# One-core hybrid decoder step: TensorE's implied waits dropped or moved, and ScalarE's bias writes moved ahead of the casts

## The chip, the cores and the metric

The kernel runs on one core of one Trainium2 chip. The metric is the device time of one execution in microseconds (us). Before the change, three runs gave a median of 1390.84 us, from 1389.94 to 1391.01.

## What is computed

One layer of a decoder for 512 prompt tokens and 8 x 4 sample tokens (544 rows of 1024 columns): windowed attention, a short convolution and memory cross-attention, an output projection, and then a mixture of 32 experts of which each token takes 4. All data is float32. The change lies in the experts alone. For the tokens of one expert the reference does this:

```
h = xb @ w_gate_up[e] + b_gate_up[e]          # 1024 -> 2048, gate and up interleaved
gate = minimum(h[:, 0::2], 7); up = clip(h[:, 1::2], -7, 7)
glu = gate * sigmoid(gate * 1.702)
out = ((up + 1) * glu) @ w_down[e] + b_down[e] # 1024 -> 1024
```

and the outputs, weighted by the gates of the router, are added to the rows of the tokens.

## The kernel before

**Staging.** After attention and router, the kernel goes through the 32 experts in order. Experts 0 to 7 and 28 to 31 are written out, 8 to 27 run in a hardware loop of five turns with four experts each. For each expert GpSimd gathers up to 104 rows of tokens from HBM (L735), TensorE transposes them (`x_rows`, L2350), and 12 MB of weights arrive in six chunks of 2 MB on SyncE's queue.

**The split of a product.** Each float32 weight is used as a high part (ScalarE's cast, `high_part`, L1096) and a low part (VectorE's difference, `low_part`, L1688, written over the raw weights). The tokens are split in the same way. A product then takes three matmuls of 512 columns: high x high, low x high, high x low (L2366, L2367, L2368).

**Halves.** A chunk is used in two halves of 12 matmuls each, so an expert has 12 halves and 144 such matmuls. TensorE's order is written out by hand in `period(n)`: the gate/up halves 0 to 5 of expert n; the activations' first transposes (`act_rows(n, 0)`, L2361) between halves 4 and 5; the next expert's `x_rows`; the down halves 6 and 7; the halves 8 and 9, which are the first two gate/up halves of expert n + 1; `act_rows(n, 1)` between 8 and 9; and the down halves 10 and 11. In the experts up to the table stage a small matmul group `info(n + 2)` (L2337) stands behind half 9. A pair of gate/up halves adds into one PSUM bank (0 to 3), the down halves into banks 4 and 5.

**Biases.** Nothing clears a bank: ScalarE copies the bias into it ahead of the matmuls (`bias_seed(n, q)`, L1134, six per expert), and all matmuls add. GpSimd spreads the bias row over the partitions beforehand (L668), and SyncE loads the next bias row when `spare_bias_in`, the count of finished bias writes, allows it.

**Waits.** Engines run their own instruction streams and meet at semaphores. TensorE waits for: `w_low` (the low part of this half), `spare_bias_in` (the bias of this bank), `x_low` and `act_low` (VectorE's low parts of the tokens and of the activations), `glu_ready` (the activations), `gathered` (the rows' transfer), `gcol_ready` (the gate column, which lies in the same bank as the transposes). Where several waits stand ahead of one instruction, one rides on the instruction itself (a weight load) and the others are instructions of TensorE's sequencer; in the hardware loop the sequencer also works out the value that is waited for.

**ScalarE's order.** `period(n)` of ScalarE goes through i = 0 to 11. In step i stands the cast of half i + 3, with the other work around it: reading the down banks (`y_rows`, i = 0), the two activation passes (`gate_over`, L1110, and `gate_sigmoid`, L1116, at i = 2 and 6), the casts of the transposes (`act_high`, L1120, at 4 and 8; `x_high`, L1125, at 6), and the six bias writes. VectorE's `low_part` of half i + 2 stands in its step i, with `clip_up`, `swiglu`, `x_low`, `act_low` around it.

Of the kernel before, what the change touches and what calls it, by code (L numbers as in the profile page):

```python
# [50 lines left out]
FROM_TABLE = 10  # L51
# [61 lines left out]
def build(nc, x_prompt, x_sample, mem_prompt, cache_win_k, cache_win_v, win_kT, mem_kT, cache_mem_v,  # L113
# [4 lines left out]
    with ctx:  # L118
# [13 lines left out]
        def sem(name):  # L132
            if name not in sems:
                sems[name] = ctx.enter_context(nc.semaphore(name))
            return sems[name]
# [279 lines left out]
        def place(n, i):  # L415
            return n * HALVES + (2 + i)
# [419 lines left out]
        def _(ac):  # L836
# [335 lines left out]
            def period(n, k, last=False):  # L1172
                for i in range(10 if last else HALVES):
                    if i == 0 and (not isinstance(n, int) or n > 0):
                        y_rows(n, k, n * HALVES + 2)
                    if i == 2:
                        gate_over(n, 0)
                        gate_sigmoid(n, 0)
                    if i == 6:
                        gate_over(n, 1)  # L1180
                        if not last:
                            x_high(n + 1)
                        gate_sigmoid(n, 1)
                    if not last or i + 3 < 10:
                        high_part(n, i + 3, last)
                    if i == 3:
                        bias_seed(n, 4)
                        bias_seed(n, 5)
                    if last and i == 5:
                        row_squares(2, 1)  # L1190
                    if last and i == 6:
                        row_squares(3, 1)
                        row_squares(4, 1)
                    if last and i == 7:
                        act_high(n, 1)
                        row_squares(0, 1)
                        row_squares(1, 1)
                    if i == 4:
                        act_high(n, 0)
                    if i == 6 and not last:  # L1200
                        bias_seed(n + 1, 0)
                    if i == 8 and not last:
                        act_high(n, 1)
                    if i >= 9 and not last:
                        bias_seed(n + 1, i - 8)

            ac.wait_ge(sem("lg_pe"), NTT)
# [694 lines left out]
        def _(pe):  # L1902
# [436 lines left out]

            def x_rows(n, k):  # L2340

                pe.wait_ge(sem("gathered"), n * 16 + 16)
                if isinstance(n, int) and n in (0, NE):
                    pe.wait_ge(sem("gcol_ready"), counted(n) + 1)
                if not isinstance(n, int) or n > 0:
                    pe.wait_ge(sem("act_low"), n * 2 - (0 if isinstance(n, int) and n == NE else 1))
                for half in range(2):
                    for q in range(4):
                        kk = half * 4 + q
                        last = tr(x_bank(half)[:, q * CAP:(q + 1) * CAP], xg[0:CAP, k % 2, kk * P:(kk + 1) * P], ident[0:CAP, 0:CAP])  # L2350
                    last.then_inc(sem("xg_pe"), 1)

            def act_rows(n, fh, overflow=False):

                pe.wait_ge(sem("glu_ready"), n * 2 + (fh + 1))
                if fh == 0 and overflow:
                    pe.wait_ge(sem("gcol_ready"), counted(n + 2))
                elif fh == 0:
                    pe.wait_ge(sem("gcol_ready"), min(n + 2, FROM_TABLE) if isinstance(n, int) else FROM_TABLE)
                for q in range(4):  # L2360
                    last = tr(banks[6 + fh][:, q * CAP:(q + 1) * CAP], up[0:CAP, fh, q * P:(q + 1) * P], ident[0:CAP, 0:CAP])  # L2361
                last.then_inc(sem("act_pe"), 1)
# [4 lines left out]
                mm(bank, low, wh, start=False, stop=False, skip_group_check=True)  # L2367
                return mm(bank, high, wl, start=False, stop=stop, skip_group_check=True)  # L2368

            def gate_up(n, i, last, k):  # L2370

                d, t = half_at(i, last)
                q = t // 2
                bank = banks[q][0:CAP, :]
                if t % 2 == 0:
                    pe.wait_ge(sem("spare_bias_in"), (n + d) * 6 + (q + 2))
                pe.wait_ge(sem("w_low"), place(n, i) + 1)
                wh, wl = split(high_w(i), 4), split(low_w(t), 4)
                for c in range(4):
                    kk = (t % 2) * 4 + c  # L2380
                    ins = products(bank, xH[:, kk, :], xL[:, kk, :], wh[:, c, :], wl[:, c, :], kk == KD - 1)
                ins.then_inc(sem("w_used"), 1)

            def down(n, i, last, middle=None):

                t = half_at(i, last)[1]
                f0 = (t - 8) * 2
                if f0 % 4 == 0:
                    pe.wait_ge(sem("act_low"), n * 2 + (f0 // 4 + 1))
                pe.wait_ge(sem("w_low"), place(n, i) + 1)  # L2390
                wh, wl = split(high_w(i), 2), split(low_w(t), 2)
                for c in range(2):
                    for dh in range(2):
                        cols = slice(dh * 512, (dh + 1) * 512)
                        ins = products(banks[4 + dh][0:CAP, :], aH[:, f0 + c, :], aL[:, f0 + c, :], wh[:, c, cols], wl[:, c, cols],
                                       f0 + c == KD - 1)
                    if c == 0 and middle:
                        act_rows(n, 1)
                ins.then_inc(sem("w_used"), 1)
# [9 lines left out]

            def period(n, k, last=False, table=False, bare=False, overflow=False):  # L2410

                gate_up(n, 0, last, k)
                gate_up(n, 1, last, k)
                gate_up(n, 2, last, k)
                gate_up(n, 3, last, k)
                gate_up(n, 4, last, k)
                act_rows(n, 0, overflow)
                gate_up(n, 5, last, k)
                if not last:
                    x_rows(n + 1, k + 1)  # L2420
                pe.wait_ge(sem("spare_bias_in"), n * 6 + 7)
                down(n, 6, last)
                down(n, 7, last, middle=last)
                if not last:
                    pe.wait_ge(sem("x_low"), n * 2 + 4)
                    gate_up(n, 8, last, k + 1)
                    act_rows(n, 1)
                    gate_up(n, 9, last, k + 1)
                    if not (table or bare):
                        info(n + 2, k)  # L2430
                down(n, 8 if last else 10, last)
                down(n, 9 if last else 11, last)
# [17 lines left out]
            head(0)  # L2450
            for u in range(2 * UB):
                period(u, u)
            with pe.Fori(2, NE // UB - 1) as it:
                for u in range(UB):
                    period(it * UB + u, u, table=True)
# [60 lines left out]
```

## Time and profile before

| | |
|---|---|
| median of three runs | 1390.84 us (1389.94 to 1391.01) |
| span of the profiled execution | 1390.0 us |
| TensorE matmul busy | 1357.6 us, 98% |
| VectorE busy | 1208.5 us, 87% |
| ScalarE busy | 1091.5 us, 79% |
| GpSimd busy | 1012.4 us, 73% |
| HBM traffic over the span | 337 GB/s |
| mean granted TensorE clock | 0.992 of full |

The profile is one execution, and its span runs from the first to the last instruction. What lies around it is not recorded, and the profiled execution has no timed value of its own: the three timed runs lie between 0.1 us below and 1.0 us above this span. A busy share is a mean over stages. A matmul's duration in the profile holds its latency, so that matmuls overlap; the distance from start to start is what a matmul costs in a stream.

### The profile page before, as it was taken

To read this page: it belongs to the slowest core of one execution; us is meant where nothing else is said; L and a number is where in the kernel's file an instruction comes from. 1 tells how busy PE (TensorE), PEld (TensorE's weight loads), DVE (VectorE), ACT (ScalarE), POOL (GpSimd) and SP (SyncE) were. 2 spreads that over 40 slices of the span, in tenths; PEclk is the share of its full clock that TensorE was granted. 3 is DMA by queue.
4 is the path that set the end of the run, shared out by engine and by line. 5 is a ranking of instruction groups with operands and counts; after the bars stand their busy time and mean duration, and the time that the engine had idled before them with its cause. 6 is when DMAs were issued, how large, how long until landed. Compare 5 with 4: busy or idle time off the path is not lost.

```text
span 1390.0 us, 19712 instructions
## 1 busy us (share of the span) xinstructions
PE 1357.6 (98%) x6762; PEld 996.9 (72%) x6762; DVE 1208.5 (87%) x1092; ACT 1091.5 (79%) x1149; POOL 1012.4 (73%) x440
## 2 busy tenths in 40 slices
PE   8999999999999999999999999999999999999995
PEld 5988656667767777777777777777777777777773
DVE  5466546899989998999999999999999999999996
ACT  5354423788879797988888888888888888888885
POOL 1122211266699999999999998899998988999943
PEclk9999998999999999999999999999999999999998
DMA  9522171999999999999999999999999999999984
GB/s 355 186 66 81 78 285 66 367 396 364 370 314 369 367 366 354 384 393 379 376 388 386 376 381 366 387 378 375 383 381 377 380 379 380 379 382 384 378 306 150
DMA packets 51802, 458.99 MB, mean 330 GB/s; under 512 B 11449, under 2 KB 15515, under 8 KB 26121
## 3 DMA queue, kind: packets, MB, share of 16 engines
q1 hardware_dynamic: 40089, 438.33, 80.5%
q0 software_dynamic: 10000, 18.19, 5.9%
q10 hardware_dynamic: 1648, 1.65, 0.4%
q8 instruction: 36, 0.59, 0.2%
q14 instruction: 29, 0.24, 0.0%
HBM read 446.62 MB, written 22.08 MB: 337 GB/s over the span
## 4 chain that ended last, share of the span: by engine, by line
PE 62%; POOL 9%; DVE 6%; issue 3%; DMA 2%; ACT 1%; POOLq 0%; ACTq 0%; DVEq 0%
PE psum L2366 20%; PE psum L2368 20%; PE psum L2367 20%; DVE low L1688 4%; POOL slot_tbl L719 3%; POOL brow L668 2%; PE psum L2350 1%; PE psum L2361 1%; DMA area<-hn_tbl,idx_i 1%; POOL y_tbl L745 1%; POOL area_r L702 1%; DMA y_tbl<-area,idx_i 1%; POOL area L735 1%; PE psum L1908 1%; POOL small L808 0%
## 5 line engine op out<-in xcount | busy, mean ns | idle before, releaser
L1688 DVE TENSOR_TENSOR low<-raw,high 128x2048 fp32r<-128x2048 f32 x384 | 874.1, 2307 | 43.1 <-ACT high L1096 42.9
L1096 ACT CAST high<-raw 128x2048 fp32r<-128x2048 f32 x384 | 727.6, 1912 | 21.1 <-PE psum L2368 15.7
L2366 PE MATMUL psum<-high,area_r 128*104 128x512 f32 x1536 | 610.4, 397 | 6.1 <-DVE low L1688 2.6
L2368 PE MATMUL psum<-low,area_r 128*104 128x512 f32 x1536 | 603.6, 393 | 0.0
L2367 PE MATMUL psum<-high,area_r 128*104 128x512 f32 x1536 | 603.2, 393 | 0.0
L668 POOL PARTITION_BROADCAST brow<-brow x192 | 345.5, 1880 | 43.6 <-DMA brow<-in_biases 35.9
L2366 PEld LDWEIGHTS psum<-high,area_r 128*104 128x104 f32 x1536 | 257.7, 168 | 101.8 <-DVE low L1688 5.5
L2368 PEld LDWEIGHTS psum<-low,area_r 128*104 128x104 f32 x1536 | 257.6, 168 | 96.3
L2367 PEld LDWEIGHTS psum<-high,area_r 128*104 128x104 f32 x1536 | 258.0, 168 | 89.9
L665 POOL COPY arrived<-cst 1x1 f32 x60 | 213.5, 3558 | 6.3 <-DMA brow<-in_biases 6.0
L735 POOL DMA_INDIRECT area<-hn_tbl,idx_i x32 | 160.1, 5004 | 74.4 <-DVE idx_i L1655 39.0
L745 POOL DMA_INDIRECT y_tbl<-area,idx_i x31 | 167.3, 5397 | 16.8 <-ACT area L1104 6.3
L1134 ACT COPY psum<-brow 104x512 f32<-104x512 f32 x192 | 110.8, 588 | 19.6 <-POOL brow L668 16.7
L645 POOL TENSOR_TENSOR ring<-ring,small 128x512 f32<-128x512 f32 (+2 forms) x18 | 24.2, 1358 | 79.9 <-DVE small L1362 79.9
L1120 ACT CAST area_r<-psum 128x416 fp32r<-128x416 f32 x64 | 32.5, 507 | 57.8 <-PE psum L2361 57.8
L1110 ACT ACTIVATE area<-psum,cst 104x512 f32<-104x512 f32 x64 | 44.1, 689 | 29.7 <-PE psum L2368 29.5
L719 POOL DMA_INDIRECT slot_tbl<-wr,us x20 | 57.4, 2871 | 5.4 <-issue 5.4
L2127 PE MATMUL psum<-ring,area 128*128 128x512 f32 x112 | 52.4, 601 | 0.0
L726 POOL CAST idx_i<-us 104x1 int32 (+1 forms) x22 | 20.4, 928 | 39.6 <-PE psum L2368 39.6
L1116 ACT ACTIVATE area<-area,cst 104x512 f32<-104x512 f32 x64 | 47.0, 734 | 2.7
L1104 ACT ACTIVATE area<-psum,area 104x512 f32<-104x512 f32 x62 | 39.3, 686 | 11.4 <-PE psum L2368 11.4
L1964 PE MATMUL psum<-area_r 128*128 128x272 f32 x160 | 47.5, 297 | 0.2 <-DVE xl L1287 0.2
(270 smaller groups left out, 1194.2 us busy)
## 6 DMA issues: line engine op xcount, KB each, us to landing
raw<-in_w_gate_up SPq DMA_DIRECT2D x128, 2048.0 KB, 12.4
raw<-in_w_down SPq DMA_DIRECT2D x64, 2048.0 KB, 12.4
ring<-in_w_in SPq DMA_DIRECT2D x7, 1024.0 KB, 15.4
ring<-in_x_prompt SPq DMA_DIRECT2D x8, 512.0 KB, 10.3
ring<-in_w_out SPq DMA_DIRECT2D x7, 512.0 KB, 4.4
ring<-in_w_mem_kv SPq DMA_DIRECT2D x2, 1024.0 KB, 9.3
ring<-in_mem_kT SPq DMA_DIRECT2D x1, 2048.0 KB, 8.6
ring<-in_cache_mem_v SPq DMA_DIRECT2D x1, 2048.0 KB, 8.5
```

The source lines that it names most:

```text
L665: nc.gpsimd.tensor_copy(arrived[0:1, part:part + 1], seen[:, bass.ds(n, 1), 0])
L668: nc.gpsimd.partition_broadcast(brow[:, cols], brow[0:1, cols], channels=P).then_inc(sem("bias_cast"), 1)
L719: nc.gpsimd.indirect_dma_start(slot_tbl[:, :], bass.IndirectOffsetOnAxis(ap=slot_i[0:n, i:i + 1].bitcast(U32), axis=0), slot_row[0:n, i, : ...
L735: nc.gpsimd.indirect_dma_start(xg[0:CAP, k % 2, :], None, hn_tbl[:, :], bass.IndirectOffsetOnAxis(ap=idx_i[0:CAP, k % UB:k % UB + 1].bitca ...
L745: nc.gpsimd.indirect_dma_start(y_tbl[:, :], bass.IndirectOffsetOnAxis(ap=idx_i[0:CAP, (k - 1) % UB:(k - 1) % UB + 1].bitcast(U32), axis=0) ...
L1096: nc.scalar.copy(high_w(i), raw_w(t)).then_inc(sem("w_high"), 1)
L1134: nc.scalar.copy(banks[q][0:CAP, :], brow[0:CAP, q * 512:(q + 1) * 512]).then_inc(sem("spare_bias_in"), 1)
L1688: v.tensor_tensor(low_w(t), raw_w(t), high_w(i), ALU.subtract).then_inc(sem("w_low"), 1)
L2127: last = mm(bank[0:n, :], zT[:, t, j * P:j * P + n], wo[t][:, half * 512:(half + 1) * 512], start=(t == tiles[0]), stop=(t == tiles[-1]))
L2366: mm(bank, high, wh, start=False, stop=False, skip_group_check=True)
L2367: mm(bank, low, wh, start=False, stop=False, skip_group_check=True)
L2368: return mm(bank, high, wl, start=False, stop=stop, skip_group_check=True)
```

## The change

On TensorE, `x_rows` no longer waits for `gathered` (but for the very first and the overflow's first); the wait stands ahead of the seventh matmul of half 5 instead. The gate/up halves no longer wait for `spare_bias_in` (but for expert 0 and the overflow's experts), nor do the down halves. Half 6 no longer waits for `act_low`; half 10 waits for `act_low` alone, and its wait for `w_low` stands ahead of the seventh matmul of half 9. `act_rows(n, 0)` no longer waits for `gcol_ready` from expert 8 on; one such wait stands ahead of the hardware loop. On ScalarE, the bias writes of banks 4 and 5 go ahead of the cast of half 6, that of bank 0 from behind the cast of half 9 to ahead of the cast of half 8, and that of bank 1 ahead of the cast of half 12 (half 0 of the next expert).

```
@@ ScalarE, period
-                    if not last or i + 3 < 10:
-                        high_part(n, i + 3, last)
                     if i == 3:
                         bias_seed(n, 4)
                         bias_seed(n, 5)
+                    if i == 5 and not last:
+                        bias_seed(n + 1, 0)
+                    if i == 9 and not last:
+                        bias_seed(n + 1, 1)
+                    if not last or i + 3 < 10:
+                        high_part(n, i + 3, last)
...
-                    if i == 6 and not last:
-                        bias_seed(n + 1, 0)
...
-                    if i >= 9 and not last:
+                    if i >= 10 and not last:
                         bias_seed(n + 1, i - 8)
@@ TensorE, x_rows
-                pe.wait_ge(sem("gathered"), n * 16 + 16)
                 if isinstance(n, int) and n in (0, NE):
+                    pe.wait_ge(sem("gathered"), n * 16 + 16)
@@ TensorE, act_rows
-                elif fh == 0:
-                    pe.wait_ge(sem("gcol_ready"), min(n + 2, FROM_TABLE) if isinstance(n, int) else FROM_TABLE)
+                elif fh == 0 and not late:
+                    pe.wait_ge(sem("gcol_ready"), n + 2)
@@ TensorE, gate_up
-                if t % 2 == 0:
+                if t % 2 == 0 and not seeded:
                     pe.wait_ge(sem("spare_bias_in"), (n + d) * 6 + (q + 2))
...
                 for c in range(4):
+                    if c == 2 and then:
+                        pe.wait_ge(sem(then[0]), then[1])
@@ TensorE, down
-                if f0 % 4 == 0:
+                if last and f0 % 4 == 0 or f0 == 4:
                     pe.wait_ge(sem("act_low"), n * 2 + (f0 // 4 + 1))
-                pe.wait_ge(sem("w_low"), place(n, i) + 1)
+                if last or f0 != 4:
+                    pe.wait_ge(sem("w_low"), place(n, i) + 1)
@@ TensorE, period
+                seeded = not overflow and not (isinstance(n, int) and n == 0)
-                gate_up(n, 0, last, k)
+                gate_up(n, 0, last, k, seeded)
...
-                gate_up(n, 2, last, k)
+                gate_up(n, 2, last, k, seeded)
...
-                gate_up(n, 4, last, k)
-                act_rows(n, 0, overflow)
-                gate_up(n, 5, last, k)
+                gate_up(n, 4, last, k, seeded)
+                act_rows(n, 0, overflow, table or bare or last)
+                gate_up(n, 5, last, k, then=None if last else ("gathered", n * 16 + 32))
...
-                pe.wait_ge(sem("spare_bias_in"), n * 6 + 7)
...
-                    gate_up(n, 8, last, k + 1)
+                    gate_up(n, 8, last, k + 1, seeded=True)
...
-                    gate_up(n, 9, last, k + 1)
+                    gate_up(n, 9, last, k + 1, then=("w_low", place(n, 10) + 1))
@@ TensorE, ahead of the hardware loop
+            pe.wait_ge(sem("gcol_ready"), FROM_TABLE)
```

## Rows read from the trace of the kernel before

**Rows 1.** Busy time by window: window, length, PE, PEld, DVE, ACT, POOL, clock, DMA share, GB/s.
```profile
273.60:360.80 87.20, 84.55 (x394) 61.60 (x393) 86.30 (x84) 73.49 (x67) 51.41 (x20) 1.00 0.98 376
361.70:567.60 205.90, 202.25 (x937) 146.74 (x936) 192.05 (x141) 174.72 (x160) 193.69 (x74) 1.00 0.96 360
563.80:1358.50 794.70, 794.70 (x3670) 584.71 (x3669) 750.86 (x505) 706.26 (x644) 702.97 (x285) 1.00 0.99 377
```

**Rows 2.** Waits from 700 to 1300 us: total, times, longest.
```profile
POOL idx_i L726 <- PE psum L2368: 33.4, 18, 2.4
DVE low L1688 <- ACT high L1096: 24.1, 17, 1.5
```

**Rows 3.** TensorE's timeline, `x_rows` of experts 10 and 31: start, duration.
```profile
598.70 0.88 PE L2350 MATMUL psum<-cst,area 104*128 104x104 f32 x8
...
1326.41 0.88 PE L2350 MATMUL psum<-cst,area 104*128 104x104 f32 x8
```

**Rows 4.** TensorE's timeline, half 11 to half 4 of the next expert, in the loop.
```profile
856.21 0.39 PE L2366 MATMUL psum<-high,area_r 128*104 128x512 f32 x1
...
858.71 0.40 PE L2368 MATMUL psum<-low,area_r 128*104 128x512 f32 x1
858.94 0.39 PE L2366 MATMUL psum<-high,area_r 128*104 128x512 f32 x1
...
861.49 0.39 PE L2368 MATMUL psum<-low,area_r 128*104 128x512 f32 x1
...
868.41 0.39 PE L2368 MATMUL psum<-low,area_r 128*104 128x512 f32 x1
...
869.77 0.40 PE L2368 MATMUL psum<-low,area_r 128*104 128x512 f32 x1
...
872.79 0.52 PE L2361 MATMUL psum<-cst,area 104*128 104x104 f32 x4
```

**Rows 5.** Sequencer instructions of TensorE by line: count, ns min/median/max, first and last start.
```profile
L2376 PEldq ALU_OP  x55: 32/32/32, 546.9 to 1212.4; - x55
L2359 PEldq EVENT_SEMAPHORE  x32: 51/51/51, 263.4 to 1353.8; - x32
L2389 PEldq EVENT_SEMAPHORE  x20: 51/51/51, 563.7 to 1221.2; - x20
L2342 PEldq FUSED_REGOPS  x20: 51/51/51, 561.0 to 1218.9; - x20
```

**Rows 6.** TensorE's and VectorE's timelines at the first gathers' landings.
```profile
270.43 0.40 PE L2368 MATMUL psum<-low,area_r 128*104 128x512 f32 x1
272.46 0.93 PE L2350 MATMUL psum<-cst,area 104*128 104x104 f32 x8 [1.63 <-DMA area<-hn_tbl,idx_i]
...
309.58 0.93 PE L2350 MATMUL psum<-cst,area 104*128 104x104 f32 x8 [1.72 <-DMA area<-hn_tbl,idx_i]
...
273.61 1.09 DVE L1752 TENSOR_TENSOR area_r<-psum,area_r 128x416 fp32r<-128x416 f32 x2 [0.92 <-ACT area_r L1125]
```

**Rows 7.** VectorE's timeline and TensorE's weight loads in half 9.
```profile
847.12 4.49 DVE L1688 TENSOR_TENSOR low<-raw,high 128x2048 fp32r<-128x2048 f32 x2
...
851.83 0.17 PEld L2366 LDWEIGHTS psum<-high,area_r 128*104 128x104 f32 x1
```

**Rows 8.** ScalarE's timeline, and VectorE's low parts of halves 5 and 6.
```profile
869.69 1.10 ACT L1134 COPY psum<-brow 104x512 f32<-104x512 f32 x2
...
853.08 0.59 ACT L1134 COPY psum<-brow 104x512 f32<-104x512 f32 x1
...
876.12 0.69 ACT L1110 ACTIVATE area<-psum,cst 104x512 f32<-104x512 f32 x1 [0.46 <-PE psum L2368]
...
868.90 4.49 DVE L1688 TENSOR_TENSOR low<-raw,high 128x2048 fp32r<-128x2048 f32 x2
```

**Rows 9.** VectorE's next low parts, and SyncE's issues: refill behind a bias load.
```profile
852.02 8.89 DVE L1688 TENSOR_TENSOR low<-raw,high 128x2048 fp32r<-128x2048 f32 x4
...
853.83 0.25 SPq L466 DMA_DIRECT2D brow<-in_biases  x1
854.34 0.33 SPq L444 DMA_DIRECT2D raw<-in_w_gate_up  x1
```

More of the change, by code:

```diff
@@ L2351, in x_rows, with act_rows @@
                     last.then_inc(sem("xg_pe"), 1)
-            def act_rows(n, fh, overflow=False):
+            def act_rows(n, fh, overflow=False, late=False):
                 pe.wait_ge(sem("glu_ready"), n * 2 + (fh + 1))
@@ L2368, in products, with gate_up @@
                 return mm(bank, high, wl, start=False, stop=stop, skip_group_check=True)
-            def gate_up(n, i, last, k):
+            def gate_up(n, i, last, k, seeded=False, then=None):
                 d, t = half_at(i, last)
@@ L2424, in period @@
                 if not last:
-                    pe.wait_ge(sem("x_low"), n * 2 + 4)
-                    gate_up(n, 8, last, k + 1)
+                    gate_up(n, 8, last, k + 1, seeded=True)
                     act_rows(n, 1)
-                    gate_up(n, 9, last, k + 1)
+                    gate_up(n, 9, last, k + 1, then=("w_low", place(n, 10) + 1))
                     if not (table or bare):
```

## The prediction

> **What bounds the kernel now.** I read the busy time by window first, then the waits, then TensorE's timeline start by start. The expert part falls into three stretches [rows 1]. From 273.6 to 360.8 us VectorE works 86.3 of 87.2 us: it sets the pace, with the slot table's work on top of its low parts. From 361.7 to 567.6 us GpSimd works 193.7 of 205.9 us, while the table is scattered. From 563.8 us until the last expert's half 4 is done, at 1358.5 us, TensorE has no idle time at all (794.7 of 794.7 us), at a granted clock of 1.00, its 2.4 GHz level. The list of waits says the same for the middle of this stretch: GpSimd and VectorE wait, and TensorE is not in the list [rows 2]. So time is to be won in the third stretch alone, and only by making TensorE's stream itself shorter. No removed wait ends a stall there.
>
> An expert costs TensorE (1326.41 - 598.70) / 21 = 34.653 us [rows 3]. Its 144 large matmuls do not all follow at one distance. Half 11 starts at 856.21 and its twelfth matmul at 858.71: 11 steps in 2.50 us, 0.227 us each. Half 0 behind it takes 858.94 to 861.49: 2.55 us, 0.232 each. Half 3 goes at 0.227 from its sixth matmul on (868.41 to 869.77, six steps in 1.36 us) [rows 4]. So the same instruction has a fast and a slow step, at one clock and without a stall.
>
> **The waits on TensorE.** Half 11 waits for `w_low` alone, and is fast. Halves 0, 2 and 4 have a second wait (`spare_bias_in`), and the stream is slow from there on; halves 1 and 3 have one wait, and the fast step comes back within them. I read this as: entering a half past a sequencer instruction that waits knocks the stream out of its fast step, and it takes more than one half to find it again. After the change halves 0 to 4 have one wait each, as half 11 has. From 858.94 to 872.79 us they take 13.85 us for 60 matmuls [rows 4]; at 0.2267 to 0.2273 us they would take 13.60 to 13.64, 0.21 to 0.25 less. I take 0.24 us per expert, with the step into half 0. The third stretch holds 794.7 / 34.65 = 23 experts, so 23 x 0.24 = 5.5 us.
>
> The bounds of this term. Below: nothing. The sequencer's instructions last 32 to 51 ns [rows 5], no view shows TensorE idle behind them, and a slow step need not come from a wait. Above: the same happens in the other halves. Outside half 11 and the fast ends of halves 1 and 3 (7 steps each), 118 of 144 matmuls are slow; 60 - 14 = 46 of them are in the forecast and 72 are not. These stand in halves 5 to 10, which start behind transposes whose waits stay, so I leave them at their step. Were half of them to become fast, 36 x 0.005 = 0.18 us more per expert, 4.1 us in all. Between the ends lies the plain price of the instructions: per expert of the loop `gathered` (51 ns), `gcol_ready` (51), `act_low` (51), four bias waits and that ahead of half 6 (32 each, 160) [rows 5] make 0.31 us, 7 us over 23 experts, if the engine paid each in full. The forecast is near the middle, and rests on what rows 4 show of a half with one wait.
>
> A rule of the Trainium skill speaks against this term. "Advanced Engine Details and Errata", section "Sequencer Loop", says that a control instruction runs in the sequencer while engine instructions already read stay queued, and "TensorE: Matmul & The Clock Gate" gives TensorE a queue of 64. By this the dropped waits were hidden, the term would be nothing, and the sum +1.4 us. The rows of the sequencer agree in part (no idle time behind them), the slow step behind doubled waits does not.
>
> **The moved wait for the gather.** `gathered` now stands ahead of the seventh matmul of half 5. In the third stretch the rows have long landed: TensorE never waits there. At 272.46 us it does: half 5's last matmul starts at 270.43, then `x_rows` waits 1.63 us for the transfer [rows 6]. In the new order TensorE stops six matmuls earlier, and these six, 6 x 0.231 = 1.4 us, come after the landing and ahead of `x_rows`. VectorE needs `x_rows` at 273.61, having waited 0.92 us through ScalarE [rows 6], and from then on it is the bound to 360.8 us, and GpSimd after it [rows 1]. Neither is shortened by TensorE, so 1.4 us are lost for good. At 309.58 us the same happens again, but there VectorE's queue, late by 1.4 us itself, covers it; without this cover it is 1.4 us more. Bounds: 0 (the transfer lands earlier) to 2.8 us.
>
> **The moved wait for the low part of half 10.** It now stands ahead of the seventh matmul of half 9, whose weight load starts at 851.83 us. VectorE ends that low part at 847.12 + 4.49 = 851.61 [rows 7]. The cover is 0.22 us, where the old place left about 1.6 (six matmuls more). I cost it at nothing: VectorE's row of work from `act_rows(n, 0)` up to there has a fixed length, and TensorE's stretch between the same points loses only what halves 5 to 9 may gain. This is the thinnest place of the change. In the first stretch VectorE has table work ahead of this low part for one expert, and TensorE will stop in half 9; VectorE is the bound there, so this costs nothing more.
>
> **The other waits.** Half 10's `act_low`, half 8's `x_low` and every half's `w_low` stay; the wait ahead of the loop is for a value that VectorE makes ahead of the low part of half 0, which TensorE awaits anyway. Nothing for these.
>
> **ScalarE's order.** The count of casts and bias writes stays. Two bias writes (1.10 us) go ahead of the cast of half 6, which then ends near 869.79 + 1.10 = 870.9 us; VectorE starts that low part at about 868.90 + 2.2 = 871.1 [rows 8]: covered by 0.2 us. The write of bank 0 (0.6 us) goes ahead of the cast of half 8, behind which `gate_over` waited 0.46 us for TensorE at 876.12 [rows 8]. Neighbours on ScalarE overlap by about 0.1, so the shift is spent there. The write of bank 1 (0.59) delays the cast of half 12, which VectorE takes as the second of the four low parts from 852.02, near 854.2 us [rows 9]; the cast would end about 853.8. Behind the earlier writes SyncE issues bias loads earlier, and with them the refill that stood behind one (853.83, then 854.34) [rows 9], by up to 0.7 us. That gains no time: the longest waits of that stretch are for computing engines, not for weights [rows 2].
>
> **The sum.** -5.5 + 1.4 = -4.1 us on the profiled span of 1390.0, to 1385.9. The median of the runs lies 0.84 above that span; I carry the difference over: 1390.84 - 4.1 = 1386.7 us.
>
> **The rivals.**
> Hidden waits: the slow step has another cause, and the stream doesn't change. For it: TensorE's sequencer works ahead, and its rows are short [rows 5]. Against it: half 11. Time: 1390.84 + 1.4 = 1392.2 us. This is also what the skill's rule gives.
> More halves turn fast: 1386.7 - 4.1 = 1382.6. Against it: transposes stay, and beyond 0.22 us between half 4 and half 9 VectorE's low part is the limit.
> Slower, the low part of half 10: a bias write of 0.58 us ahead of `x_high` delays VectorE's `x_low` by as much, if the wait of 0.46 us does not absorb it. Then TensorE stops in every half 9, for 0.58 - 0.22 = 0.36 us, 23 x 0.36 = 8.3 us: 1390.84 + 1.4 + 8.3 = 1400.5. It decides as soon as that low part comes 0.22 us later against TensorE than now; a delay of 0.4 us would already outweigh the forecast's gain. Against it: the 0.46 us.
> Transfers become the bound: the DMA engines are busy 0.99 in the third stretch [rows 1]. What is left, 0.01 x 34.65 = 0.35 us per expert, is more than 0.24, but barely. If they hold back half the gain: 1386.7 + 2.7 = 1389.4.
>
> **How the numbers follow.** Chances: forecast 0.48, hidden waits 0.27, more halves 0.10, slower 0.10, transfers 0.05. A difference under 0.2% (2.8 us) is about what a measurement of this kernel can't tell from no change: from 1388.1 to 1393.6. The forecast's own range is 1384.5 to 1389.0; a seventh of it (0.07) lies inside that band. Faster: 0.41 + 0.10 + 0.02 = 0.53. Same: 0.07 + 0.25 + 0.03 = 0.35. Slower: 0.10, and 0.02 of the hidden waits, if the gather costs twice: 0.12. The range reaches from 1382.0, in the middle of the case of more halves, to 1393.0, over the case of hidden waits; the slower case and the edges, 0.2, are left out.
>
> **What would show it.** Right: `x_rows` from 598 us on at a distance of 34.4 us in place of 34.65; halves 0 to 4 at 0.227 us throughout; TensorE still without idle time from about 565 us; the second `x_rows` (272.46 before) near 273.9, with the six matmuls behind the landing. Wrong: halves 0 to 4 at 0.232 as before (hidden waits); TensorE waiting for VectorE's low part in half 9 in each expert, or idle time of VectorE ahead of `x_low` (slower); ScalarE's casts waiting for weights late in the loop (transfers).

## The result, and the profile after

The changed kernel takes 1396.05 us (median of five runs, 1395.61 to 1398.44), the kernel before beside it 1389.94 (1388.77 to 1391.01): a ratio of 1.005, 95% interval 1.0040 to 1.0061, or 6.1 us slower. I had forecast 4.1 us faster. The profiled execution of after is the run of 1396.05 us; its span is 1394.3, so that the time lies 1.75 us above the span, as it does in the other four runs within 0.1. By that measure the profile of before, with its span of 1390.0, was a run of about 1391.8, itself 1.8 above its median. The two profiles therefore show only 4.3 of the 6.1 us.

Busy time by window, after (columns as in [rows 1], the same windows):

```profile
273.60:360.80 87.20, 81.85 (x379) 59.87 (x378) 82.98 (x81) 69.35 (x64) 48.91 (x21) 0.98 0.95 351
361.70:567.60 205.90, 202.98 (x940) 147.67 (x939) 194.57 (x142) 175.66 (x160) 190.24 (x72) 1.00 0.97 364
563.80:1358.50 794.70, 794.55 (x3667) 583.82 (x3666) 748.77 (x505) 703.52 (x643) 714.09 (x286) 1.00 0.99 377
```

The loss is visible in the first stretch: VectorE, which sets the pace there, works 82.98 us where it worked 86.30, and the DMA engines move 351 GB/s where they moved 376. The third stretch, where I wanted to win, looks nearly as before.

TensorE's timeline, after: `x_rows` of experts 10, 29, 30 and 31 (L2352 is L2350 of before):

```profile
602.33 0.88 PE L2352 MATMUL psum<-cst,area 104*128 104x104 f32 x8
...
1260.74 0.88 PE L2352 MATMUL psum<-cst,area 104*128 104x104 f32 x8
1295.78 0.88 PE L2352 MATMUL psum<-cst,area 104*128 104x104 f32 x8
1330.74 0.88 PE L2352 MATMUL psum<-cst,area 104*128 104x104 f32 x8
```

From 602.33 to 1260.74 an expert takes 658.41 / 19 = 34.653 us, to the nanosecond what it took before [rows 3]. The last two distances are 35.04 and 34.96. So from expert 10 on the loop neither gained nor lost; the last experts lost 0.7 us up to 1330.74; and `x_rows` of expert 10 is already 3.6 us late (598.70 before).

The timelines of TensorE, VectorE, ScalarE and SyncE, after, around half 5 of experts 0 and 1:

```profile
269.81 0.40 PE L2370 MATMUL psum<-low,area_r 128*104 128x512 f32 x1
272.39 0.48 PE L2368 MATMUL psum<-high,area_r 128*104 128x512 f32 x1 [2.19 <-DMA area<-hn_tbl,idx_i]
...
273.87 0.88 PE L2352 MATMUL psum<-cst,area 104*128 104x104 f32 x8
...
307.43 0.40 PE L2370 MATMUL psum<-low,area_r 128*104 128x512 f32 x1
312.66 0.75 PE L2368 MATMUL psum<-high,area_r 128*104 128x512 f32 x1 [4.84 <-DMA area<-hn_tbl,idx_i]
313.21 0.63 PE L2369 MATMUL psum<-high,area_r 128*104 128x512 f32 x1
...
314.92 0.63 PE L2370 MATMUL psum<-low,area_r 128*104 128x512 f32 x1
315.34 1.15 PE L2352 MATMUL psum<-cst,area 104*128 104x104 f32 x8
...
315.58 0.69 DVE L1765 TENSOR_SCALAR area<-psum 104x512 f32<-104x512 f32 x1 [2.46 <-PE psum L2370]
...
271.20 0.59 ACT L1134 COPY psum<-brow 104x512 f32<-104x512 f32 x1 [1.44 <-POOL brow L668]
...
315.57 0.33 SPq L444 DMA_DIRECT2D raw<-in_w_gate_up  x1
```

At the first landing it went as forecast: six matmuls behind it, `x_rows` at 273.87 (272.46 before [rows 6]). At the second it did not. TensorE stands for 4.84 us (1.72 before), then takes its six matmuls at 0.43 us each instead of 0.23, and `x_rows` starts at 315.34 (309.58 before). VectorE, which I had counted on to cover this, waits 2.46 us, and not for `x_rows`: its instruction at L1765 is `clip_up` of expert 1 itself, which reads the sums of half 5. And SyncE's next refill goes out at 315.57: it waits until half 5 has used its weights, and half 5 now ends behind the gather. SyncE's timeline, before:

```profile
307.90 0.33 SPq L444 DMA_DIRECT2D raw<-in_w_gate_up  x1
```

Busy time by window over these 8 us, before and then after:

```profile
307.40:315.40 8.00, 6.28 (x33) 4.48 (x32) 7.90 (x10) 5.94 (x8) 7.09 (x6) 1.00 1.00 416
```

```profile
307.40:315.40 8.00, 3.16 (x9) 1.86 (x8) 5.59 (x7) 3.00 (x4) 6.15 (x5) 0.82 0.78 258
```

The weights' stream, full before, falls to 0.78, and the granted clock to 0.82: TensorE had been standing for 4.84 us, and from 312.66 to 315.34, where its matmuls are 0.43 us apart, the granted clock is 0.50, the 1.2 GHz level.

### The profile page after: what moved, and what is told of

Read it like the earlier page. It is cut to its first block, busy times and chain, and to the rows that moved or that the text cites. A ratio compares the mean times of both kernels' runs of the same rounds, so it can differ in the third digit from the quotient of the medians.

```text
span 1394.3 us, 19471 instructions
## 1 busy us (share of the span) xinstructions
PE 1356.7 (97%) x6762; PEld 994.2 (71%) x6762; DVE 1210.2 (87%) x1092; ACT 1089.7 (78%) x1149; POOL 1018.3 (73%) x440
## 4 chain that ended last, share of the span: by engine, by line
PE 62%; DVE 9%; POOL 5%; DMA 3%; issue 3%; ACT 1%; POOLq 0%; ACTq 0%; DVEq 0%
PE psum L2368 20%; PE psum L2370 20%; PE psum L2369 20%; DVE low L1690 6%; DMA area<-hn_tbl,idx_i 3%; POOL brow L668 2%; POOL slot_tbl L719 2%; PE psum L2363 1%; PE psum L2352 1%; DVE area_r L1754 1%; DVE area L1772 1%; DVE area L1775 0%; POOL area_r L702 0%; POOL small L808 0%; DVE area L1765 0%
## 5 line engine op out<-in xcount | busy, mean ns | idle before, releaser
L668 POOL PARTITION_BROADCAST brow<-brow x192 | 363.3, 1973 | 39.8 <-DMA brow<-in_biases 29.7
L665 POOL COPY arrived<-cst 1x1 f32 x60 | 201.1, 3352 | 0.3
L1765 DVE TENSOR_SCALAR area<-psum 104x512 f32<-104x512 f32 x64 | 43.9, 685 | 5.2 <-PE psum L2370 3.2
```

The lines of the kernel that those rows point to most:

```text
L665: nc.gpsimd.tensor_copy(arrived[0:1, part:part + 1], seen[:, bass.ds(n, 1), 0])
L668: nc.gpsimd.partition_broadcast(brow[:, cols], brow[0:1, cols], channels=P).then_inc(sem("bias_cast"), 1)
```

## The experiments

Each ratio is against runs of the kernel before on the same chip, with its 95% interval; 0.1% is 1.4 us.

**The parts alone.** Three kernels add one part to the kernel before; a fourth takes the two moved waits out of the changed kernel.

The gather's wait alone (in `x_rows`, `gate_up` and `period`):
```
-                pe.wait_ge(sem("gathered"), n * 16 + 16)     # x_rows, but for n in (0, NE)
+                    if c == 2 and then:                      # gate_up
+                        pe.wait_ge(sem(then[0]), then[1])
-                gate_up(n, 5, last, k)
+                gate_up(n, 5, last, k, then=None if last else ("gathered", n * 16 + 32))
```


> The kernel before, with the wait for the gathered rows moved into half 5 and nothing else. Theory (the gather's wait in the first experts is the loss): the second x_rows 1.4 us later than before, the third about 315 us in place of 309.6, TensorE idle for several us inside half 5 of expert 1; the distance of x_rows in the loop stays 34.653; in all 4 to 5.5 us slower than before. Rival (the loss is the wait for the low part of half 10, or ScalarE's order): 0 to 1.4 us slower.

Measured: 1.0018 (1.0007 to 1.0029), 2.5 us. The loop stays at 34.653. In its profile the second gather landed early, TensorE stood for only 0.54 us in half 5 of expert 1, and `x_rows` followed at 310.38, so this profile shows the wait where it is cheap. The wait is a part of the loss, not all of it.

The wait for the low part of half 10 alone (in `period` and `down`; `gate_up` as above):
```
-                    gate_up(n, 9, last, k + 1)
+                    gate_up(n, 9, last, k + 1, then=("w_low", place(n, 10) + 1))
-                pe.wait_ge(sem("w_low"), place(n, i) + 1)
+                if last or f0 != 4:
+                    pe.wait_ge(sem("w_low"), place(n, i) + 1)
```


> The kernel before, with the wait for the low part of half 10 moved into half 9 and nothing else. Theory: free in the loop (34.653 us per expert stays), some 0.3 us in each of the last three experts and under 1 us in the first ones, 0.5 to 1.5 us slower in all. Rival (this wait is the loss): 4 to 6 us slower.

Measured: 1.0015 (1.0005 to 1.0025), 2.1 us, between the two; 34.653 from expert 10 on, 35.03 in the last experts. In experts 0 to 3 half 9 shows no stall. It has one in experts 4, 6 and 8, where I expected none. Timelines of VectorE and TensorE in expert 4 of this kernel, the low part of half 10 and the sixth and seventh matmul of half 9:

```profile
429.05 4.49 DVE L1688 TENSOR_TENSOR low<-raw,high 128x2048 fp32r<-128x2048 f32 x2
...
432.64 0.39 PE L2368 MATMUL psum<-low,area_r 128*104 128x512 f32 x1
433.60 0.48 PE L2366 MATMUL psum<-high,area_r 128*104 128x512 f32 x1 [0.56 <-DVE low L1688]
```

From `x_rows` of expert 4 to that of expert 10 this kernel takes 218.10 us, the first profile of before 217.05, with the same distance of 38.42 from expert 4 to 5 in both. The gather's wait back, below, against the dropped waits with ScalarE's order gives the same: 215.16 against 214.28.

ScalarE's order alone (the first hunk of the diff and its counterparts, all waits kept):

> The kernel before, with ScalarE's bias writes ahead of the casts and every wait of TensorE kept. Theory: no difference that can be measured, within 1 us of before, with ScalarE's waits for GpSimd (1.4 and 1.7 us in the first experts of the changed kernel) hidden behind VectorE's queue. Rival (ScalarE's order delays the low parts of the first experts): 1.5 to 3 us slower, x_low of the second expert later by that.

Measured: 1.0011 (0.9997 to 1.0025), 1.5 us, which doesn't decide; in its profile VectorE waits 0.86 us for `x_high` of the second expert, no more than before (0.92 [rows 6]).

The dropped waits and ScalarE's order (both moved waits put back):

> The changed kernel with both moved waits put back, so the dropped waits and ScalarE's order alone. Theory (dropped waits were hidden): 34.653 us per expert as before, time within 1 us of before. My forecast's own step (each dropped second wait gives back the fast step): 34.41 us per expert, 5.5 us faster than before. Rival (ScalarE's order costs): 1.5 to 3 us slower than before.

Measured: 1.0013 (1.0002 to 1.0024), and 34.653 us per expert. My forecast's step, 34.41, is refuted: dropping the second waits gives nothing. The sequencer's instructions had really gone. The line of the wait for `spare_bias_in`, L2376 before, has 55 ALU_OP rows in the loop [rows 5] and none here. In the written-out experts the wait for `w_low` behind it becomes one that rides on its weight load. Sequencer rows of that line, before, then in this kernel:

```profile
L2377 PEldq EVENT_SEMAPHORE  x48: 51/51/1435, 244.6 to 1352.8; - x48
...
L2379 PEldq EVENT_SEMAPHORE  x4: 51/51/1745, 244.7 to 262.8; - x4
```

And half 0, which has one wait in the changed kernel, as half 11 has, keeps its slow step there, 2.55 us from the first to the twelfth matmul. TensorE's timeline, after:

```profile
862.58 0.39 PE L2368 MATMUL psum<-high,area_r 128*104 128x512 f32 x1
...
865.13 0.39 PE L2370 MATMUL psum<-low,area_r 128*104 128x512 f32 x1
```

**The changed kernel and its undoings.** Unaltered, then with the gather's wait back, then with the low part's wait back (the diffs above, reversed).

> The changed kernel, unaltered, beside its own partial undoings. Theory (the losses add up: 2.7 us for the gather's wait, 2.2 for the low part of half 10, 1.3 for the rest, each by the medians of the runs with one part alone): 6 us slower than before. Rival (the two moved waits make each other worse in the first experts, the stall in half 5 of expert 1 being long enough for the granted clock to fall): 6 us as well, but then its two undoings give back more than their own parts.

> The changed kernel with the gather's wait back ahead of x_rows. Theory (losses add up): 2.7 us below the changed kernel, 3.5 us above before; the last three experts still stall 0.3 to 0.4 us each in half 9. Rival (the two waits make each other worse): 4 us or more below the changed kernel, 1 to 2 us above before.

> The changed kernel with the wait for the low part of half 10 back ahead of half 10. Theory (losses add up): 2.2 us below the changed kernel, 4 us above before; no stall in half 9 of any expert, the six matmuls of half 5 still behind the landings. Rival (the two waits make each other worse): 3.5 us or more below the changed kernel.

Measured: 1.0051 (1.0032 to 1.0071), 1.0030 (1.0017 to 1.0042), 1.0018 (1.0004 to 1.0032). The gather's wait back recovers 0.21%, the low part's 0.33%. Alone they cost 0.18% and 0.15%; with intervals of 0.1% and more on either side this neither needs nor excludes a mutual worsening. (By the marks set beforehand the first, 2.9 us, fits losses that add up, and the second, 4.6 us, its rival, which asked for 3.5 or more.) What the profiles do show is that the price of the gather's wait differs between them. GpSimd's timelines, the gather of expert 2, in after, then in the kernel with the gather's wait alone:

```profile
289.27 9.93 POOL L735 DMA_INDIRECT area<-hn_tbl,idx_i  x1 [13.62 <-DVE idx_i L1657]
```

```profile
288.86 7.49 POOL L735 DMA_INDIRECT area<-hn_tbl,idx_i  x1 [14.77 <-DVE idx_i L1655]
```

The same instruction takes 9.93 or 7.49 us. In the three profiles with the moved wait and about 9.93 us (after, its repetition, and the low part's wait back) TensorE stood for 4.84, 4.90 and 4.24 us in half 5, and the DMA share from 307.4 to 315.4 us was 0.78, 0.78 and 0.80. In the two with the moved wait and 7.5 us (the gather's wait alone, and the kernel of the last experts below) it stood for 0.54 us and not at all, at a share of 1.00 and 1.01. `x_rows` of expert 4 then starts at 386.7 to 387.1 us in the three and at 383.0 and 384.7 in the two; in the thirteen profiles without this wait in the first experts it starts at 380.8 to 383.9. Whether the kernel or the single execution decides between 9.93 and 7.5 is open: only before and after were profiled twice, with 9.93 or 9.94 each time.

**More waits.** The kernel before, with each half's wait repeated ahead of every third matmul:
```
                 for c in range(4):                           # gate_up, and the like in down
+                    if c:
+                        pe.wait_ge(sem("w_low"), place(n, i) + 1)
```


> The kernel before with 28 more waits per expert on TensorE: each half's wait for its low part repeated, with its register arithmetic, ahead of every third matmul. Theory (the sequencer works ahead, such waits are hidden): 34.65 us per expert in the loop, the same steps in halves 0 to 4 and 11, time within 1 us of before. My forecast's step (a second wait knocks the stream out of its fast step): half 11 and the fast ends of halves 1 and 3 turn slow, 26 steps by 0.005 us, 34.77 us per expert, 2.8 us slower. Plain price of 51 ns a wait: 36.1 us per expert, over 30 us slower.

Measured: 1.0005 (0.9991 to 1.0018). There are 36 more waits per expert, not the 28 of my text (3 in each of 12 halves). They are not sequencer instructions: the rows of line L2377 are as many as before (48 EVENT_SEMAPHORE, 140 ALU_OP), so no register arithmetic was added either, and nothing stands at the new lines: each rides on its weight load. This run therefore tests a satisfied wait on a weight load, and not the sequencer instruction that my forecast was about. TensorE's timeline of this kernel, `x_rows` of experts 10 and 31, then the first and twelfth matmul of half 11 and of half 0:

```profile
599.54 0.88 PE L2350 MATMUL psum<-cst,area 104*128 104x104 f32 x8
...
1327.26 0.88 PE L2350 MATMUL psum<-cst,area 104*128 104x104 f32 x8
...
857.06 0.39 PE L2366 MATMUL psum<-high,area_r 128*104 128x512 f32 x1
...
859.55 0.40 PE L2368 MATMUL psum<-low,area_r 128*104 128x512 f32 x1
859.79 0.39 PE L2366 MATMUL psum<-high,area_r 128*104 128x512 f32 x1
...
862.34 0.39 PE L2368 MATMUL psum<-low,area_r 128*104 128x512 f32 x1
```

727.72 / 21 = 34.653 again. Half 11 keeps its fast step (2.49 us for 11 steps) with three waits inside it, half 0 its slow one (2.55). A satisfied wait cost this stream nothing, neither where the sequencer's instructions were taken away (the dropped waits, above) nor where one was added to a weight load.

**Where the loss lies.** The changed kernel with both moved waits in the hardware loop only (one of its four hunks):
```
-                gate_up(n, 5, last, k, then=None if last else ("gathered", n * 16 + 32))
+                gate_up(n, 5, last, k, then=None if last or isinstance(n, int) else ("gathered", n * 16 + 32))
```


> The changed kernel with both moved waits only in the hardware loop (experts 8 to 27); in the written-out experts they stand where they stood before. Theory (the whole loss lies in the first experts, at the gathers' landings, and in half 9 of the last three): 34.653 us per expert from the tenth to the last, no stall in half 5 of experts 0 and 1 beyond before's, 0 to 2 us slower than before. Rival (the moved waits cost in the loop as well, by a lasting lag of the buffers behind them): 4 us slower or more.

Measured: 1.0018 (1.0006 to 1.0031), 2.5 us: 34.653 from expert 10 on, but from `x_rows` of expert 9 to that of expert 10, 35.68 us against 34.92 before, and more is left than I had put down for ScalarE's order.

The last experts: there GpSimd's broadcast has no small copy ahead of it, as it has in the loop.
```
-                if not isinstance(n, int):
+                if not isinstance(n, int) or n > NE - UB:
                     seen = cst[...]
                     nc.gpsimd.tensor_copy(arrived[0:1, part:part + 1], ...)
```


> The changed kernel, with GpSimd's small copy that stands ahead of the bias broadcast in the hardware loop also in the last experts. Theory (the low part of half 10 lasts 2.95 us in place of 2.28 in the last three experts because GpSimd's broadcast starts just ahead of it, and half 9 waits for it): low part 2.28 us, no stall in half 9 of experts 28 to 30, 34.653 us per expert to the end, 1.1 us below the changed kernel, 5 to 6 us above before. Rival (the low part is late for another reason): 35.03 us for the last experts as in the changed kernel, no gain.

Measured: 34.653 to the end, 1.0044 (1.0027 to 1.0061). The timelines of VectorE, GpSimd and TensorE in expert 28, first of after, then of this kernel:

```profile
1259.22 2.95 DVE L1690 TENSOR_TENSOR low<-raw,high 128x2048 fp32r<-128x2048 f32 x1
...
1267.21 4.49 DVE L1690 TENSOR_TENSOR low<-raw,high 128x2048 fp32r<-128x2048 f32 x2
...
1259.12 3.71 POOL L668 PARTITION_BROADCAST brow<-brow  x2
...
1271.30 0.40 PE L2370 MATMUL psum<-low,area_r 128*104 128x512 f32 x1
1271.75 0.48 PE L2368 MATMUL psum<-high,area_r 128*104 128x512 f32 x1
```

```profile
1259.61 2.28 DVE L1690 TENSOR_TENSOR low<-raw,high 128x2048 fp32r<-128x2048 f32 x1
...
1259.47 0.61 POOL L665 COPY arrived<-cst 1x1 f32<-1x1 f32 x1
1259.63 3.59 POOL L668 PARTITION_BROADCAST brow<-brow  x2
```

In after the broadcast starts 0.10 us ahead of the low part of half 7, which then lasts 2.95 us. Everything behind it on VectorE shifts, half 10's low part ends at 1267.21 + 4.49 = 1271.70, and TensorE's seventh matmul of half 9 comes at 1271.75, 0.45 us behind the sixth. With the copy the broadcast starts 0.02 us behind the low part, which lasts 2.28, and the stall is gone. The low part of 2.95 us stands in VectorE's timeline of before as well; there nothing waited for it:

```profile
1255.58 2.95 DVE L1688 TENSOR_TENSOR low<-raw,high 128x2048 fp32r<-128x2048 f32 x1
```

**What makes the slow step, then?** The kernel before in three variants: one more increment on the ninth matmul of each half, no stop flags, and the first two matmuls of a product exchanged (here the first, in `gate_up`, and the like in `down`; the others are edits of `products`). Each was executed once, for its profile, so their times are not compared:
```
+                    if c == 2:
+                        ins.then_inc(sem("ninth"), 1)
```

> The kernel before, with one more semaphore increment on the ninth matmul of every half. What breaks the fast step? Theory (the increment on a half's last matmul does): half 11 and the fast ends of halves 1 and 3 break at the ninth matmul, 15 or so steps by 0.005 us lost, 34.7 us per expert. Rival (it is not the increment): the steps as before, 34.653.

> The kernel before with the stop flag left off the last matmul of each sum. Theory (the flag at the end of halves 1, 3 and 11 adds the 8 ns there and ends the fast step): the fast step goes on into halves 0, 2 and 4, 34.4 us per expert or a little more. Rival (it is not the flag): the steps as before, 34.653.

> The kernel before, with the three matmuls of a product in another order (low part of the tokens first). Does the order in which operands are read set the slow step? Theory (the step follows the sequence of operands): another pattern of steps in halves 0 to 4 and 11, and another time per expert. Rival (it does not): 34.653 us and the same steps.

Measured: 34.653 us per expert in all three, with every step where it was. Neither the waits, an added increment, the stop flags nor the order of these two matmuls set it.

**ScalarE's order, placed.** The whole change from expert 8 on alone; the kernel before unaltered, as a yardstick; and the kernel before with ScalarE's new order in experts 0 to 7 alone. The middle of the first (`early` is "expert 0 to 6"; in the last it selects the experts from 8 on):
```
+                    if early:
+                        high_part(n, i + 3, last)
                     if i == 3:
                         bias_seed(n, 4)
                         bias_seed(n, 5)
+                    if i == (6 if early else 5) and not last:
                         bias_seed(n + 1, 0)
                     if i == 9 and not last:
                         bias_seed(n + 1, 1)
+                    if not early and (not last or i + 3 < 10):
                         high_part(n, i + 3, last)
```


> The whole change from expert 8 on alone (the two moved waits only in the hardware loop); experts 0 to 7 as before, TensorE's waits and ScalarE's order both. Theory (all of the loss lies in the first experts and in half 9 of the last three): 34.653 us per expert, within 1 us of before. Rival (ScalarE's order or the moved waits cost something in the loop or at the end too): 1.5 to 3 us slower, as with the moved waits in the loop alone.

> The kernel before, unaltered, under the same treatment as the others. Any theory: no difference from before; what it shows apart from zero is the reach of such a comparison, and its profile a second view of the first experts.

> The kernel before, with ScalarE's new order in experts 0 to 7 alone. Theory (ScalarE's order costs in the first experts, where a bias write waits for GpSimd's broadcast and the cast behind it with it): 1 to 2 us slower. Rival (ScalarE's order costs nothing, the 0.11% measured with it alone was spread): within 0.7 us of before.

Measured: 1.0003 (0.9993 to 1.0013), 1.0011 (0.9998 to 1.0024) and 1.0015 (1.0006 to 1.0023). The yardstick says that a single figure of 0.11% means nothing by itself; their medians are 1389.70, 1389.38 and 1391.84 beside 1389.24. From expert 8 on the change costs nothing that the times show. The profile of that first kernel shows one place where the loop pays: in expert 8, the first of the loop, half 9 waits for the low part, and the two distances of `x_rows` from expert 9 to 11 are together 70.40 us against 69.57 before. TensorE's timeline of this kernel, sixth and seventh matmul of half 9:

```profile
574.58 0.39 PE L2374 MATMUL psum<-low,area_r 128*104 128x512 f32 x1
575.55 0.48 PE L2372 MATMUL psum<-high,area_r 128*104 128x512 f32 x1 [0.58 <-DVE low L1693]
```

ScalarE's order in the first experts alone measured about 2 us, at the edge of what the yardstick lets one say. Timelines of that last kernel, ScalarE, VectorE and GpSimd in expert 0:

```profile
272.42 0.59 ACT L1134 COPY psum<-brow 104x512 f32<-104x512 f32 x1 [4.46 <-POOL brow L668]
272.94 1.91 ACT L1096 CAST high<-raw 128x2048 fp32r<-128x2048 f32 x1
...
275.33 0.89 ACT L1125 CAST area_r<-psum 128x416 fp32r<-128x416 f32 x2
...
275.86 1.09 DVE L1757 TENSOR_TENSOR area_r<-psum,area_r 128x416 fp32r<-128x416 f32 x2 [3.54 <-ACT area_r L1125]
...
269.54 3.52 POOL L668 PARTITION_BROADCAST brow<-brow  x2 [10.34 <-DMA brow<-in_biases]
```

The bias row of expert 1 comes late: GpSimd waits 10.34 us for its transfer, ScalarE 4.46 us for GpSimd, with the cast of half 8, `gate_over` and `x_high` queued behind, and VectorE 3.54 us for `x_high` (0.92 before [rows 6]). In the old order this write stood behind the casts of halves 8 and 9. This profile is of a run of 1393.87 us, near the slow end of its kernel, and the wait isn't there in each: of the nine profiles with the new order in expert 0, VectorE waits for `x_high` for 3.54 and 2.41 us in two and for at most 0.86 in seven; in the nine with the old order, for at most 1.56. So the path is shown, its usual price is not.

## Why the prediction was wrong

**What bounds the kernel**: right for the third stretch. TensorE has next to no idle time there before or after (794.55 of 794.70 us), so only its own stream could win.

**The waits on TensorE, -5.5 us**: this step failed. It measured 0. I read the neighbourhood of slow step and second wait as a cause. Dropping the waits refutes it (34.653, with half 0 as slow as before); the added waits, which ride on weight loads, show only that such waits cost nothing (34.653, with half 11 still fast). After itself shows the reverse too. Behind the stall of half 9 in expert 28, half 11, with its one wait, takes 2.55 us instead of 2.50; TensorE's timeline, first and twelfth matmul:

```profile
1276.01 0.39 PE L2368 MATMUL psum<-high,area_r 128*104 128x512 f32 x1
...
1278.56 0.39 PE L2370 MATMUL psum<-low,area_r 128*104 128x512 f32 x1
```

So the same half with the same wait goes at either step, after a different entry. What sets it is open. The rival of hidden waits was right about this term, and the short rows of the sequencer [rows 5], which I had as the lower bound, were the evidence to weigh more. The Trainium skill's rule ("Advanced Engine Details and Errata", section "Sequencer Loop"), by which other engine instructions can be read and queued while a control instruction executes, agrees with this trace: the removed waits changed 34.653 us by nothing.

**The other waits, nothing**: right in effect, but misread. Half 8's wait for `x_low` does not stay: `period` drops it too, in a line between those that the diff above shows. VectorE makes that value ahead of the low part of half 8, for which TensorE waits anyway.

**The gather, +1.4 us**: the first place was right, the size wrong; alone it measured 2.5 us. At the first landing `x_rows` came 1.41 us later, as in the sum. At the second the cover that I named, VectorE's queue, was not there, and three things that I hadn't priced came together: a later landing, six matmuls at half the clock (2.68 us from 312.66 to 315.34, not 1.4), and a refill held back until 315.57. The last is the most general: in `x_rows` the wait held back nothing but `x_rows`; inside half 5 it holds the buffer that half 5 uses, and the sums that ScalarE and VectorE read next.

**The low part of half 10, nothing**: wrong, 2.1 us alone, and the profile of that kernel places about all of it. One us lies between `x_rows` of experts 4 and 10 (218.10 against 217.05): the stalls of half 9 in experts 4, 6 and 8, two of them in the second stretch, for which I had no price because I looked at this wait only in the loop and in the first stretch. Behind expert 8 the cover of 0.22 us [rows 7] held. The other, 0.75 us in two distances of 35.03 and a last stall, lies in the last three experts. I had called VectorE's row of work up to there of fixed length; in them it is 0.67 us longer (in after, distances of 0.38 and 0.31 us more, and a like stall in expert 30), and the kernel with the copy has none of these stalls at the end. In the first experts half 9 stalls only in kernels that have ScalarE's new order as well (in after 0.7 and 0.3 us in experts 1 and 2: the seventh matmul comes 0.90 and 0.53 us behind the sixth; in its repetition not at all); this was not taken apart further. My slower rival named this very wait, but laid it in each expert and to ScalarE's order. On the longer low part a page of the Trainium skill, "SBUF — State Buffer", section "Who interferes with whom", states that a VectorE instruction with two SBUF inputs contends with a GpSimd instruction that reads SBUF, and that issue order decides who blocks. The two starts, 0.10 us apart in after and reversed by the copy, agree with that. The low part grew by 0.67 us, far less than the broadcast's 3.7 for two.

**ScalarE's order, nothing**: right for the loop; in expert 0 I had costed the shifts of casts, not what the moved instruction itself waits for, up to 4.46 us. What that costs is not settled: 2.1 us (0.15%) in the first experts by the times, beside a yardstick of 0.11%, and the long wait for `x_high` in two of nine profiles.

**The sum**: 2.5 + 2.1 + 2.1 = 6.7 us against 6.1 measured, and 0.03% for the same change from expert 8 on. Each term is uncertain by some 1.5 us, so the agreement of the sum is partly luck; that TensorE's stream gained nothing, and that nearly all of the loss lies in the first ten and the last three experts, is not. No version with repeated runs was faster than the kernel before.

## What to carry to other kernels

A moved wait must be priced at what its instruction waits for in the slowest place it runs, here the first experts where transfers land late, and at everything queued behind it on its engine. A wait put inside a unit of work also holds that unit's buffers and results, and with them the refills and the engines that read next. Two steps of different length that stand beside a wait are no proof that the wait makes them: a kernel with that wait alone taken out is a cheap test, and a wait that is added must be looked up in the profile, since it may ride on another instruction and test something else.

## What the runs showed of the hardware

The granted clock fell at the second gather in the unaltered kernel's other profile too. Busy time by window and TensorE's timeline of that run:

```profile
307.40:315.40 8.00, 5.23 (x18) 4.04 (x18) 7.74 (x10) 4.60 (x6) 7.09 (x6) 0.63 0.97 409
```

```profile
310.27 1.65 PE L2350 MATMUL psum<-cst,area 104*128 104x104 f32 x8 [2.77 <-DMA area<-hn_tbl,idx_i]
...
312.14 0.63 PE L2367 MATMUL psum<-high,area_r 128*104 128x512 f32 x1
312.56 0.63 PE L2368 MATMUL psum<-low,area_r 128*104 128x512 f32 x1
```

After 2.77 us of waiting the matmuls go at 0.42 us. But here they stand behind `x_rows`, the DMA share stays at 0.97, and VectorE is busy for 7.74 of 8 us. The fall may still cost something (the next `x_rows` comes after 37.99 us, after 36.95 in the first profile of before, with other differences between the two); what the change did was to put the wait and the slow matmuls ahead of the sums and the refill that others wait for.

GpSimd's share of time varies between executions of one kernel: the distance of `x_rows` from expert 4 to 5, where the table is scattered, is 38.42 us in the first profile of before and 36.24 in the second, which is as much as any part of this change is worth.
